# Causal attention in split precision: value products of two heads at a time, exponentials three steps ahead, and the low halves of the outputs added by VectorE

## The chip, the cores and the metric

The kernel runs on one core of a Trainium2 chip. The time is device microseconds of one execution; three executions of the kernel before were timed, and one more was recorded by the hardware profiler. The engines are TensorE (PE in the profile), its weight loads (PEld), VectorE (DVE), ScalarE (ACT), GpSimd (POOL), and SyncE (SP), which starts the DMAs.

## What is computed

A trunk of two layers over 1024 tokens of width 1024, in float32. The first layer splits its input projection between latent attention and a state-space branch; the second is gated linear attention. Only the attention of the first layer is touched:

```
q = (rms_norm(cq) @ w_uq)      -> 8 heads of 64 + 32 rotary columns
k, v from rms_norm(ckv) @ w_ukv, 8 heads of 64 each, shared rotary key of 32
s = (q_nope @ k_nope.T + q_rope @ k_rope.T) * 96**-0.5, causal
o = softmax(s) @ v             -> (1024, 8*64)
o_mla = o * silu(g_mla)
y = concat(o_mla, o_s5) @ w_out
x1 = layer_norm(alpha * x + y)
```

## The kernel before, in words

**Steps.** Attention runs over 64 steps n. A step is one tile i of 128 queries and one head h; pair p holds the tiles 2p and 2p + 1, and n = 16p + 2h + t for the tile 2p + t. The scores of a step are 128 queries by (i + 1) x 128 keys. Steps with i < 4 (n < 32, pairs 0 and 1) are SHORT: their scores fit one PSUM bank. The others take two banks.

**What happens to one step**, each item on another engine, in this order:

- "s": PE multiplies queries and keys (L2028) and adds the causal bias in the last block (L2032). VectorE takes the negated row maximum (`score_max`, L1678).
- `exponentials`: ScalarE turns the scores into probabilities in SBUF, with the row sum (L1247). This frees the score bank.
- "pt": PE transposes the probabilities block by block into bank 4 or 5 (L1950). ScalarE copies them in a rounded form, the high part (L1286); VectorE subtracts that from the same bank to get the low part (L1753). This frees the bank.
- "av": for both tiles of a head at once PE multiplies the high and the low part of the probabilities by the head's values (L2168). The stationary operand is 128 columns wide: 64 high and 64 low columns of the values, for an odd head in the opposite order. An even head writes columns 0 to 255 of bank 7, the odd head after it columns 256 to 511. So 64 of the 128 output rows are the product with the high halves of the values and the other 64 that with the low halves, and both have to be added.

**An output turn** ends each two heads, 16 times (j = 0 to 15), at the steps in `OUTPUT_TURNS` (6, 10, ..., 30, then 32, 36, ..., 60). In it VectorE scales the gate rows by the inverse sums (`gate_scaled`, L1710 and L1712); PE transposes them into bank 6 ("gT", L1950 on gate); ScalarE copies these to gateT (L1295) and bank 7 to o_parts (`output_parts`, L1268). PE multiplies o_parts by a matrix of shifted ones and adds the result to bank 7 ("ob", L2177 and L2179): this brings the low halves to the rows of the high ones. VectorE multiplies the sum in bank 7 by gateT and writes OT, which shares memory with gate (`output_gated`, L1722 and L1723). Only then is bank 7 free for the next "av".

**Other work in the loop.** "q" multiplies out the queries of later tiles (L1941) and "qT" transposes them; both use bank 6, as "gT" does. GpSimd turns the queries (L729 to L734), splits the values (L1040), and later splits the weights of the output projection (L1022, L1023). `mix_hi_tile` and `mix_lo_tile` split gated outputs for that projection.

**What sets the order.** One generator, `attention_steps`, gives the order of the items; PE, ScalarE and VectorE each run through it and issue in order what is theirs. `PsumPlan` gives each job its bank and semaphore: PE waits in `claim` until the job before on that bank is drained. The items between one "pt" and the next were placed by hand. Before, the exponentials of step n + 1 are issued around the high part of step n, and the high part of the even step that reuses one of three cells waits for the value product that read it (`values_done`).

**Behind the loop** PE runs the last "av" and "gT", the output projection of tile 0 ("z0", 36 products), and then the last "ob". SyncE waits until the last `output_gated` has drained bank 7 before it loads the weights of the layer norm into ln_gb (L907), which lies over o_parts and gateT. GpSimd applies them (L1065, L1066), and PE transposes the result.

## Time and profile before

| | us |
|---|---|
| median of three runs | 938.72 |
| lowest and highest | 937.49, 941.99 |
| the profiled execution | 938.28 |
| its span | 936.6 |
| PE busy in the span | 856.3 (91%) |
| VectorE busy | 596.9 (64%) |
| ScalarE busy | 381.6 (41%) |
| GpSimd busy | 258.1 (28%) |

The time is that of the whole execution, the span that from the first to the last instruction recorded. The mean clock that TensorE was granted is 0.966 of full speed; 1.0 stands for 2.4 GHz and 0.5 for 1.2 GHz. Attention takes the stretch from about 200 to 432 us. Busy shares over the whole span say little of one stage, so the rows below are read stage by stage. A matmul's end is modelled: where PE is full, what one instruction costs is read from one start to the next.

### The profile page before, as it was taken

The numbers are of one execution on the slowest core, as the hardware profiler recorded it, in microseconds if no ns is written. First come the engines' busy times: TensorE is split into PE (matmuls) and PEld (weight loads), VectorE is DVE, ScalarE is ACT, GpSimd is POOL, SyncE is SP. The second block draws the span as 40 slices with busy tenths as digits, with TensorE's granted clock in tenths as the row PEclk, the third lists the DMA queues.
The fourth block names the chain that finished last, engine by engine and source line by source line (L and its number), as shares of the span: only waits on it lengthen the run. The fifth ranks groups of instructions, "written<-read, shape, count | busy, mean of one in ns | idle before, by whom it ended". The sixth has DMA issues, their size and how long they took to land.

```text
span 936.6 us, 12171 instructions
## 1 busy us (share of the span) xinstructions
PE 856.3 (91%) x4136; PEld 679.3 (73%) x4136; DVE 596.9 (64%) x983; ACT 381.6 (41%) x731; POOL 258.1 (28%) x259
## 2 busy tenths in 40 slices
PE   7999999987777989998899899999899999999995
PEld 6898775755445666667787588888678888888884
DVE  6988789455444676773687154368996676654453
ACT  6253325654344555661323265325433546221120
POOL 2000002612020182000696633001955013142243
PEclk9999999996798999998999999999999999999998
DMA  9011265000000030003422311033733223012111
GB/s 330 23 28 41 70 86 119 24 3 1 1 1 1 1 113 1 1 1 116 132 90 91 112 45 46 1 112 102 213 113 123 79 68 136 23 65 71 46 45 67
DMA packets 40685, 64.19 MB, mean 69 GB/s; under 512 B 8256, under 2 KB 21824, under 8 KB 40608
## 3 DMA queue, kind: packets, MB, share of 16 engines
q1 hardware_dynamic: 40624, 63.42, 22.4%
q8 instruction: 33, 0.54, 0.2%
q14 instruction: 28, 0.23, 0.1%
HBM read 52.33 MB, written 9.44 MB: 66 GB/s over the span
## 4 chain that ended last, share of the span: by engine, by line
PE 58%; DVE 22%; ACT 7%; issue 7%; DMA 3%; POOL 1%; SPq 1%; DVEq 0%; ACTq 0%; POOLq 0%
PE psum L1941 32%; PE psum L2255 15%; PE psum L1950 4%; PE psum L2028 4%; DVE probT_lo L1753 2%; DVE negmax L1678 2%; PE psum L2168 2%; DMA ln_gb<-ln_b_dram 1%; PE psum L1976 1%; ACT probT_hi L1286 1%; ACT prob L1247 1%; DVE vg_lo L1813 1%; DMA wgs_raw<-even_w_in_dram 1%; DMA xT_raw<-x_cols_dram 1%; DVE x_lo_raw L1845 1%
## 5 line engine op out<-in xcount | busy, mean ns | idle before, releaser
L1753 DVE TENSOR_TENSOR probT_lo<-psum,probT_hi 128x512 fp32r<-128x512 f32 (+2 forms) x96 | 53.5, 558 | 63.1 <-ACT probT_hi L1286 60.8
L2255 PE MATMUL psum<-vg_hi,x1T_hi 128*128 128x512 f32 x208 | 82.1, 395 | 5.5 <-DVE vg_lo L1813 5.5
L2255 PE MATMUL psum<-vg_lo,x1T_hi 128*128 128x512 f32 x208 | 81.7, 393 | 0.0
L2255 PE MATMUL psum<-vg_hi,x1T_lo 128*128 128x512 f32 x208 | 81.6, 392 | 0.0
L2028 PE MATMUL psum<-kT,qTt 96*128 96x512 f32 (+2 forms) x192 | 79.8, 529 | 0.1
L1286 ACT ACTIVATE probT_hi<-psum 128x512 fp32r<-128x512 f32 (+2 forms) x96 | 47.1, 490 | 63.1 <-PE psum L1950 59.8
L1678 DVE TENSOR_REDUCE negmax<-psum 128x1 f32<-128x128 f32 (+3 forms) x64 | 48.5, 758 | 22.5 <-PE psum L2032 21.2
L1247 ACT ACTIVATE prob<-psum,negmax 128x128 f32<-128x128 f32 (+3 forms) x64 | 47.4, 740 | 32.5 <-issue 25.9
L2168 PE MATMUL psum<-probT_hi,V 128*128 128x256 f32 (+1 forms) x160 | 44.2, 307 | 14.2 <-DVE gate L1723 9.7
L1950 PE MATMUL psum<-ident,prob 128*128 128x128 f32 x288 | 48.5, 299 | 9.4 <-DVE probT_lo L1753 5.3
L1065 POOL TENSOR_TENSOR zn<-zn,ln_gb 128x512 f32<-128x512 f32 x16 | 23.1, 1443 | 106.9 <-DMA ln_gb<-ln_b_dram 92.6
L2168 PEld LDWEIGHTS psum<-probT_hi,V 128*128 128x128 f32 x160 | 33.5, 209 | 24.0 <-DVE gate L1723 15.7
L1941 PE MATMUL psum<-w_out_hi,Y1T_hi 128*128 128x512 f32 x128 | 50.6, 395 | 0.0
L2028 PEld LDWEIGHTS psum<-kT,qTt 96*128 96x128 f32 x192 | 35.9, 210 | 20.1 <-issue 16.4
L2255 PEld LDWEIGHTS psum<-vg_hi,x1T_hi 128*128 128x128 f32 x208 | 39.3, 189 | 15.1 <-DVE vg_lo L1813 6.8
L1941 PE MATMUL psum<-w_out_hi,Y1T_lo 128*128 128x512 f32 x128 | 49.9, 390 | 0.0
L1941 PE MATMUL psum<-x1T_hi,wqk_lo 128*128 128x512 f32 x128 | 49.9, 390 | 0.0
L1941 PE MATMUL psum<-x1T_lo,wqk_hi 128*128 128x512 f32 x128 | 49.9, 390 | 0.0
L1941 PE MATMUL psum<-w_out_lo,Y1T_hi 128*128 128x512 f32 x128 | 49.9, 389 | 0.0
L1941 PE MATMUL psum<-x1T_hi,wqk_hi 128*128 128x512 f32 x128 | 49.8, 389 | 0.0
L1950 PEld LDWEIGHTS psum<-ident,prob 128*128 128x128 f32 x288 | 33.5, 151 | 19.8 <-issue 9.8
L2255 PEld LDWEIGHTS psum<-vg_hi,x1T_lo 128*128 128x128 f32 x208 | 39.5, 190 | 8.2
(404 smaller groups left out, 2201.3 us busy)
## 6 DMA issues: line engine op xcount, KB each, us to landing
vg_piece<-odd_w_in_dram SPq DMA_DIRECT2D x60, 256.0 KB, 3.2
x_res<-x_dram SPq DMA_DIRECT2D x8, 512.0 KB, 4.2
wqk_raw<-odd_w_in_dram SPq DMA_DIRECT2D x8, 512.0 KB, 5.1
x_scratch<-zn SPq DMA_DIRECT2D x8, 512.0 KB, 2.9
w_out_raw<-odd_w_out_dram SPq DMA_DIRECT2D x4, 1024.0 KB, 5.0
V<-x_scratch SPq DMA_DIRECT2D x8, 512.0 KB, 4.6
out_dram<-SG SPq DMA_DIRECT2D x8, 512.0 KB, 2.9
xT_raw<-x_cols_dram SPq DMA_DIRECT2D x7, 512.0 KB, 8.6
```

The source lines that it names most:

```text
L1065: step(pool.tensor_tensor(zn[:, i % 2, s], zn[:, i % 2, s], ln_gb[:, 0, s], ALU.mult))
L1247: step.frees(act.activation(prob[:, place:place + (i + 1) * P], src, ACT.Exp, bias=negmax[:, n % 4:n % 4 + 1], accum_out=rsum[:, i % 2, h: ...
L1286: step(act.activation(hi, source, ACT.Copy), prob_hi_set)
L1678: step(vec.tensor_reduce(negmax[:, n % 4:n % 4 + 1], scores(n)[0], AX_X, ALU.max, negate=True), max_set)
L1753: step.frees(vec.tensor_tensor(lo, source, hi.bitcast(F32), ALU.subtract), ("pt", number))
L1813: step(vec.tensor_tensor(vg_lo[n % 3][:, :], vg_raw(n), vg_hi[n % 3][:, :].bitcast(F32), ALU.subtract), vg_split)
L1845: step(vec.tensor_tensor(lo, hi, a_lo, ALU.add), rows_summed)
L1941: mm = pe.matmul(out, lhsT, rhs, start=(k == 0), stop=(k == len(pairs) - 1))
L1950: mm = pe.transpose(bank(*job)[0:rows, k * P:k * P + cols], block_in, identity[0:cols, 0:cols])
L2028: mm = pe.matmul(psum[:, slot + part, 0:c1 - c0], qTt[:, i % 2, h, :], kT[:, h, c0:c1], start=True, stop=not diag, skip_group_check=diag)
L2168: mm = pe.matmul(bank("o", n // 2)[:, c0 + t0 * P:c0 + 2 * P], V[k][:, h // 2, 2 * (h % 2):2 * (h % 2) + 2, :].rearrange("p s d -> p (s d) ...
L2255: mm = pe.matmul(bank(*job), lhsT, rhs, start=(k == 0 and j == 0 and product not in ADDS_TO), stop=(k == 3 and j == len(pairs) - 1), skip_ ...
```

## The change

- **Low halves.** The shift matrix, o_parts and the step "ob" on PE go. `output_parts` copies only the low halves from bank 7, each to the rows of its high halves (o_low, two copies of 64x256). `output_gated` adds them to the high halves in the bank (two instructions of 64x256, into o_sum) and multiplies o_sum by gateT in one instruction of 128x256. The name "ob" stays for the job of the odd head on bank 7.
- **Value products in the short pairs.** Both heads of a turn are multiplied out in one place, ahead of "pt" at n = 5, 9, 13, ..., 29 and 32, where before each had a place of its own (n = 3, 5, 7, ...). Their places in the long pairs stay.
- **Output turns.** "gT" moves behind the scores of its step in all pairs. In the short pairs `gate_scaled` moves to the end of the step before and `output_gated` behind the low part of the step after. `output_parts` moves behind the high parts.
- **Exponentials.** In the short pairs those of step n + 3 follow the high part of step n; in the long pairs they stay as they were.
- **Queries.** The places of "q" and "qT" move by a step or so.

```diff
-        o_parts = at("o_parts", ln_at, [P, 512], F32R)
+        o_low, o_sum = at("o_low", ln_at, [P, 2 * P]), at("o_sum", ln_at + 512, [P, 2 * P])
...
         def values_turn(n):
-            return n > 2 and n % 2 == int(n in SHORT)
+            if n == len(SHORT) or n % 4 == 1 and n in SHORT:
+                return ((n - 4) // 4 * 2, (n - 4) // 4 * 2 + 1)
+            if n % 2 == 0 and n - 2 not in SHORT:
+                return (n - 2) // 2,
+            return ()
+        def queries_at(p, r):
+            places = (3, 4, 5, 7) if p else (0, 1, 3, 4)
+            if p < 3 and r in places:
+                return (2 * p + 2 + places.index(r) // 2, places.index(r) % 2),
+            return ()
...
             for n, (i, h) in enumerate(heads):
                 p, r = divmod(n, 16)
-                if values_turn(n):
-                    yield "av", (n - 2) // 2
+                for m in values_turn(n):
+                    if m >= 0:
+                        yield "av", m
                 yield "pt", n
-                if n in OUTPUT_TURNS:
-                    yield "gT", OUTPUT_TURNS.index(n)
-                    yield "ob", OUTPUT_TURNS.index(n)
-                if p and r in (1, 2):
-                    yield "qT", (2 * p + r - 1, 1)
-                if p < 3 and r in (10, 11):
-                    yield "qT", (2 * p + r - 8, 0)
-                if p < 3 and r in ((3, 5, 6, 7) if p else (0, 1, 2, 3)):
-                    nth = ((3, 5, 6, 7) if p else (0, 1, 2, 3)).index(r)
-                    yield "q", (2 * p + 2 + nth // 2, nth % 2)
+                if p and r in (0, 1):
+                    yield "qT", (2 * p + r, 1)
+                if p < 3 and r in (9, 11):
+                    yield "qT", (2 * p + 2 + (r == 11), 0)
+                for key in queries_at(p, r):
+                    yield "q", key
                 if n + 4 in SHORT:
                     yield "s", n + 4
                 if n + 2 < len(heads) and n + 2 not in SHORT:
                     yield "s", n + 2
+                if n in OUTPUT_TURNS:
+                    yield "gT", OUTPUT_TURNS.index(n)
             yield "av", STEPS - 1
             yield "gT", STEPS // 2 - 1
             yield "z0", 0
-            yield "ob", STEPS // 2 - 1
...
             def output_parts(j):
-                plan.filled(act, ("o", j))
-                step.frees(act.activation(o_parts[:, :], bank("o", j), ACT.Copy), ("o", j))
+                plan.filled(act, ("ob", j))
+                step(act.activation(o_low[0:VD, :], bank("o", j)[VD:P, 0:2 * P], ACT.Copy))
+                step.frees(act.activation(o_low[VD:P, :], bank("o", j)[0:VD, 2 * P:4 * P], ACT.Copy), ("o", j))
...
                 elif what == "pt":
-                    if n % 2 == 0 and n >= 4:
+                    if n % 2 == 0 and n + 1 not in SHORT:
                         exponentials(n + 1)
-                    if n in OUTPUT_TURNS:
-                        output_parts(OUTPUT_TURNS.index(n))
...
                         step(act.activation(hi, source, ACT.Copy), prob_hi_set)
-                    if n % 2 and 4 <= n + 1 < len(heads):
+                    if 4 <= n + 3 and n + 3 in SHORT:
+                        exponentials(n + 3)
+                    if n % 2 and n + 1 < len(heads) and n + 1 not in SHORT:
                         exponentials(n + 1)
+                    if n in OUTPUT_TURNS:
+                        output_parts(OUTPUT_TURNS.index(n))
...
-            step(vec.tensor_copy(shift[:, 0:VD], ident[:, VD:2 * VD]))
-            step(vec.tensor_copy(shift[:, 2 * VD:3 * VD], ident[:, 0:VD]))
-            step(vec.tensor_tensor(shift[:, VD:2 * VD], ident[:, 0:VD], ident[:, 0:VD], ALU.subtract))
...
             def output_gated(j):
                 p, k = divmod(j, 4)
-                plan.filled(vec, ("ob", j))
+                plan.drained(vec, ("o", j))
+                src = bank("ob", j)
+                step(vec.tensor_tensor(o_sum[0:VD, :], src[0:VD, 0:2 * P], o_low[0:VD, :], ALU.add))
+                step(vec.tensor_tensor(o_sum[VD:P, :], src[VD:P, 2 * P:4 * P], o_low[VD:P, :], ALU.add))
                 plan.drained(vec, ("gT", j))
-                cols = slice(2 * p * P, 2 * (p + 1) * P)
-                src = bank("ob", j)
-                step(vec.tensor_tensor(OT[0:VD, k, cols], src[0:VD, 0:2 * P], gateT[j % 2][0:VD, :], ALU.mult))
-                step.frees(vec.tensor_tensor(OT[VD:P, k, cols], src[VD:P, 2 * P:4 * P], gateT[j % 2][VD:P, :],
+                step.frees(vec.tensor_tensor(OT[:, k, 2 * p * P:2 * (p + 1) * P], o_sum[:, :], gateT[j % 2][:, :],
                                              ALU.mult), ("ob", j))
...
                 elif what == "pt":
-                    if n in OUTPUT_TURNS:
+                    if n in OUTPUT_TURNS and n not in SHORT:
                         gate_scaled(OUTPUT_TURNS.index(n))
-                    if n - 1 in OUTPUT_TURNS:
+                    if n - 1 in OUTPUT_TURNS and n - 1 not in SHORT:
                         output_gated(OUTPUT_TURNS.index(n - 1))
...
                         step.frees(vec.tensor_tensor(lo, source, hi.bitcast(F32), ALU.subtract), ("pt", number))
+                    if n + 1 in OUTPUT_TURNS and n + 1 in SHORT:
+                        gate_scaled(OUTPUT_TURNS.index(n + 1))
+                    if n - 1 in OUTPUT_TURNS and n - 1 in SHORT:
+                        output_gated(OUTPUT_TURNS.index(n - 1))
...
-                elif what == "ob":
-                    plan.claim(pe, ("ob", n))
-                    pe.matmul(bank("ob", n)[0:VD, 0:2 * P], shift[:, 0:VD], o_parts[:, 0:2 * P],
-                              start=False, stop=True, skip_group_check=True)
-                    pe.matmul(bank("ob", n)[:, 2 * P:4 * P], shift[:, VD:3 * VD], o_parts[:, 2 * P:4 * P],
-                              start=False, stop=True, skip_group_check=True).then_inc(plan.full(("ob", n)), 1)
```

## Rows read from the trace of the kernel before

**Rows 1.** By stretch: start:end length, busy PE, PEld, DVE, ACT, POOL, clock, DMA, GB/s.

```profile
199.90:214.71 14.81, 11.59 (x59) 7.90 (x59) 8.61 (x22) 8.90 (x28) 7.56 (x14) 0.98 0.00 1
214.71:226.29 11.58, 8.97 (x34) 6.60 (x34) 5.00 (x14) 4.34 (x14) 3.21 (x3) 0.50 0.01 1
226.29:237.47 11.18, 8.33 (x34) 5.58 (x34) 5.80 (x13) 4.35 (x14) 0.00 (x0) 0.78 0.00 0
237.47:251.18 13.71, 9.94 (x44) 5.94 (x44) 7.55 (x14) 5.84 (x14) 0.00 (x0) 0.77 0.00 0
251.18:268.07 16.89, 13.52 (x58) 9.11 (x58) 6.65 (x13) 7.52 (x17) 2.80 (x6) 0.88 0.00 1
268.07:282.33 14.26, 10.49 (x54) 6.73 (x54) 7.13 (x13) 6.54 (x15) 2.75 (x6) 0.88 0.00 1
282.33:294.95 12.62, 8.82 (x46) 6.78 (x46) 6.15 (x11) 6.05 (x14) 0.00 (x0) 0.86 0.01 1
294.95:305.94 10.99, 10.06 (x51) 7.15 (x52) 4.90 (x9) 5.48 (x12) 0.00 (x0) 0.84 0.00 0
```

**Rows 2.** Tile gate, its groups (ns min/median/max), then who waited (us, times).

```profile
L1712 DVE TENSOR_TENSOR gate<-gate,rinv x16: 424/426/2432, 212.0 to 429.6; 128x256 f32<-128x256 f32 x16
L1723 DVE TENSOR_TENSOR gate<-psum,gateT x16: 427/427/428, 214.3 to 441.8; 64x256 f32<-64x256 f32 x16
...
  PEld psum L2168: 15.7, 10
  PEld psum L1950: 12.5, 10
```

**Rows 3.** Tile o_parts: the copy's group, then who waited for it.

```profile
L1268 ACT ACTIVATE o_parts<-psum x16: 597/597/598, 211.9 to 433.3; 128x512 fp32r<-128x512 f32 x16
...
  PEld psum L2177: 6.6, 8
```

**Rows 4.** Timeline of PE in pair 1 (start, us, instruction, [idle before]).

```profile
269.56 1.46 PE L1941 MATMUL psum<-w_uq,cT 128*128 128x384 f32 x4
270.85 1.02 PE L2028 MATMUL psum<-kT,qTt 96*128 96x512 f32 x2
...
271.77 0.50 PE L1950 MATMUL psum<-ident,prob 128*128 128x128 f32 x3
272.10 0.81 PE L2028 MATMUL psum<-kT,qTt 96*128 96x384 f32 x2
...
272.78 0.36 PE L2168 MATMUL psum<-probT_hi,V 128*128 128x256 f32 x1
...
273.75 0.62 PE L1950 MATMUL psum<-ident,prob 128*128 128x128 f32 x4
274.21 1.02 PE L2028 MATMUL psum<-kT,qTt 96*128 96x512 f32 x2
```

**Rows 5.** Timeline, the turn at 381 us.

```profile
381.89 0.33 PE L2177 MATMUL psum<-o_parts,shift 128*64 128x256 f32 x1 [0.71 <-ACT o_parts L1268]
...
382.18 1.67 PE L2028 MATMUL psum<-kT,qTt 96*128 96x512 f32 x4
```

**Rows 6.** Timeline, GpSimd and VectorE at 346 us.

```profile
346.71 2.34 POOL L1023 TENSOR_TENSOR w_out_lo<-w_out_raw,w_out_hi 128x1024 fp32r<-128x1024 f32 x1
...
346.90 2.43 DVE L1712 TENSOR_TENSOR gate<-gate,rinv 128x256 f32<-128x256 f32 x1
```

**Rows 7.** Timelines of VectorE, GpSimd and PE behind attention.

```profile
441.31 0.42 DVE L1722 TENSOR_TENSOR gate<-psum,gateT 64x256 f32<-64x256 f32 x1 [11.24 <-PE psum L2179]
...
447.67 0.81 DVE L1462 TENSOR_SCALAR zn<-zn,stat 128x1024 f32<-128x1024 f32 x1
...
448.80 1.53 POOL L1065 TENSOR_TENSOR zn<-zn,ln_gb 128x512 f32<-128x512 f32 x1 [92.58 <-DMA ln_gb<-ln_b_dram]
...
451.79 0.66 PE L1950 MATMUL psum<-ident,zn 128*128 128x128 f32 x4 [2.39 <-POOL zn L1066]
...
453.75 0.63 PE L1941 MATMUL psum<-w_out_hi,OT_lo 128*128 128x512 f32 x1
```

More of the change, by code:

```diff
@@ L270, in hybrid_trunk @@
         OT_lo = at("OT_lo", RC + 4096, [P, H * VD // P, S], F32R)
-        o_parts = at("o_parts", ln_at, [P, 512], F32R)
+        o_low, o_sum = at("o_low", ln_at, [P, 2 * P]), at("o_sum", ln_at + 512, [P, 2 * P])
         gateT = [at(f"gateT{s}", ln_at + 1024 + 256 * s, [P, 2 * P]) for s in range(2)]
-        shift = at("shift", RB + 7168, [P, 3 * VD], F32R)
         gs5_lo = at("gs5_lo", D6, [P, 2, S], F32R)
@@ L489, in scores @@
             return psum[:, b0:b0 + len(score_banks(n)), :].rearrange("p a b -> p (a b)")[:, 0:w], b0 * 512
-        OUTPUT_TURNS = [4 * j + (6 if 4 * j + 5 in SHORT else 4) for j in range(STEPS // 2 - 1)]
+        OUTPUT_TURNS = [4 * j + (6 if 4 * j + 6 in SHORT else 4) for j in range(STEPS // 2 - 1)]
         def values_turn(n):
-            return n > 2 and n % 2 == int(n in SHORT)
+            if n == len(SHORT) or n % 4 == 1 and n in SHORT:
[8 more added lines that the diff above has]
+            return ()
         def attention_steps():
@@ L530, in hybrid_trunk @@
                     plan.give(("pt", number), 4 + number % 2)
-            elif what == "av" and n % 2 == 0:
-                plan.give(("o", n // 2), 7)
-            elif what == "ob":
-                plan.give(("ob", n), 7)
+            elif what == "av":
+                plan.give(("ob" if n % 2 else "o", n // 2), 7)
             elif what == "z0":
@@ L710, in hybrid_trunk @@
         for m, g in cell_users:
-            if m % 2 == 0 or (m, g + 1) in cell_of:
+            if (m, g + 1) in cell_of:
                 value_turns[m, g] = len(value_turns) + 1
@@ L718, in values_done @@
             else:
-                plan.filled(engine, ("o", m // 2))
+                plan.filled(engine, ("ob" if m % 2 else "o", m // 2))
         def prob_blocks(n, number, first, blocks):
@@ L902, in _ @@
                 if i == 1:
-                    plan.filled(sp, ("o", STEPS // 2 - 1))
+                    plan.filled(sp, ("ob", STEPS // 2 - 1))
                     wqk_load(0)
@@ L2173, in _ @@
                         if k == 2 * p + 1 or k % 4 == 3:
-                            mm.then_inc(pv_done if (n, k // 4) in value_turns else plan.full(("o", n // 2)), 1)
-                elif what == "ob":
-                    plan.claim(pe, ("ob", n))
-                    pe.matmul(bank("ob", n)[0:VD, 0:2 * P], shift[:, 0:VD], o_parts[:, 0:2 * P],
-                              start=False, stop=True, skip_group_check=True)
-                    pe.matmul(bank("ob", n)[:, 2 * P:4 * P], shift[:, VD:3 * VD], o_parts[:, 2 * P:4 * P],
-                              start=False, stop=True, skip_group_check=True).then_inc(plan.full(("ob", n)), 1)
+                            mm.then_inc(pv_done if (n, k // 4) in value_turns
+                                        else plan.full(("ob" if h % 2 else "o", n // 2)), 1)
                 elif what == "gT":
```

## The prediction

> **What bounds the kernel now.** I went from the page's 40 slices (the granted clock leaves full speed in the slices that belong to attention's first half) to the view by stretches, cut at each end of L1723, the last instruction of an output turn [rows 1]. A step is one query tile of one head; each row but the first and the last is four steps, the first seven, the last two. Steps 0 to 15 are pair 0 (128 and 256 keys), steps 16 to 31 pair 1 (384 and 512). The reader should see that no other engine is full in these eight rows, and that behind the first the clock is granted at 0.50 to 0.88: VectorE (DVE) is busy 5.00 of 11.58 us, 5.80 of 11.18, 7.55 of 13.71, 6.65 of 16.89, ScalarE (ACT) no more. TensorE (PE) looks busy because at half clock its instructions last longer. So the stretch from 200 to 306 us is a chain of waits. Who waits for whom is in the view of the tile gate [rows 2]: the weight loads of the value products wait 15.7 us in ten places for L1723, those of the gate transposes 12.5 us in ten for L1712; and the shift products 6.6 us in eight for ACT's copy [rows 3]. The order of the work makes it: gate scaling, transpose, copy, shift product and gating stand within one step, each on another engine, and the next value product is queued right behind on PE.
>
> **The sum is against the profiled execution,** 938.28 us (span 936.6), which is 0.44 below the median of 938.72.
>
> **Removed: the shift product and its copy.** Sixteen pairs of products go. A pair costs PE 0.29 us of queue (381.89 to the next score product at 382.18) and before it the wait, 0.71 there [rows 3, 5]. ACT's copy of 128x512, 0.597, becomes two of 64x256; the nearest row is the 128x256 copy of gateT, 0.38, so ACT pays 0.8 for 0.6: +0.2 per turn. The three constants for the shift at 170 us go too; nothing waits for them, and I count nothing.
>
> **Added on DVE.** Before: two products of 64x256, 0.43 each (L1723; L1722 is like it) [rows 2]. After: two adds of the same shape and sources, and a product of 128x256 from two SBUF tiles, like L1712, 0.43. So +0.45 per turn, 7 us in 16 turns; it costs nothing where DVE has idle time, which it has in all short rows, and its full size where DVE is the late one.
>
> L1712 took 2.43 us once, at 346.90, with GpSimd's split running from 346.71 to 349.05 [rows 6]: the new product can be held up as L1712 was. Two turns (L1722 at 336 and 352 us now) lie beside those splits: at worst 2 us each, at best nothing; I take 1.5 us together. The Trainium skill (SBUF — State Buffer, "SBUF: two separate sides") says that a VectorE instruction with two SBUF inputs and a GpSimd instruction exclude each other for a whole instruction. By it the two adds, which read PSUM, are safe and the product is not; the old gating, PSUM times SBUF, was never exposed. The L1712 row agrees for its kind; the sum above stands on the row alone.
>
> **Moved, in the short pairs.** Gate scaling goes a step earlier (after the low part of step 5, 9, ...), the transpose behind the score of step 6, 10, ..., the gating behind the low part of step 7, 11, ..., and the value products of both heads to step 9, 13, .... The wait for L1712 should vanish: half a step or more now lies between. The wait for the gating shrinks, since a transpose and a score product stand before the value product, but does not vanish. Exponentials run three steps ahead instead of one, so that transposes no longer wait for ACT. What is late next: DVE's run of low part, three gating instructions, maximum; then ACT, where the exponential of n+3 sits between the high parts of n and n+1 and waits for a maximum queued behind the gating.
>
> Full-clock cost on PE, start to start [rows 4]: query product 1.29, score of 512 keys 0.92, of 384 keys 0.68, transposes of three blocks 0.33 and of four 0.46, value product 0.97. Four steps of pair 1: 2 x (0.92 + 0.68 + 0.33 + 0.46 + 0.97) + 0.25 for the gate = 7.0 us. With the queries in between (some 0.5 per turned half, an estimate from 0.11 a block): 237.47 to 251.18: 8; to 268.07: 7.0 + 4 x 1.3 = 12.2; to 282.33: 9; to 294.95, where two steps have no score: 6; the two steps to 305.94, with five and six blocks: 6. Sum 41 us against 68.5 on the clock. The best of these rows now runs at 16.89/12.2 = 1.38 times its need, with its stalls. I take 1.35 for all: 55.5 us, **gain 13**. Bounds: 1.2 (gain 19) and 1.55 (gain 5). DVE's busy time, 32.4 us plus 5 x 0.45, stays below in each case.
>
> Pair 0: the two four-step rows take 22.8 us. If only DVE counted they would be 5.0 + 0.45 and 5.8 + 0.45, some 6 us each; if PE stayed at half clock, its busy time there, 9.0 [rows 1], is nearly full. I take 8.5 each, since an engine that has to stop for latencies will see the lower clock again: gain 5.8 (between 4 and 10). The first seven steps lose one wait of L1723 and one of L1712 and keep four query products: 1.2. **Gain 7.**
>
> **Long pairs (306 to 432 us).** The turn at 381 us [rows 5]: the score product comes 1.0 us sooner (0.71 + 0.29), so the maximum that waits for it can start some 0.8 sooner. Behind it on DVE stand gating and the low part of the next step, and for these the value product waits. Gating is 0.45 longer: 0.4 remains. Seven turns: 2.8. If DVE has no slack beside it: minus 0; if PE is the late one: up to 7. Less the 1.5 above: **gain 1.3.**
>
> **Behind attention.** The last shift product stands behind 36 products of the output projection; DVE sits idle 11.24 us for it until 441.31, and only then are the layer norm's weights asked for; GpSimd waits for them until 448.80, PE for GpSimd 2.39 us until 451.79, and PE then runs eight products at 1.2 GHz (0.63 us each, starts some 0.4 apart) [rows 7]. After: the gating ends near 435.5 (copy 433.3 to 434.1, then 1.3), the weights come 6.7 us sooner, and the layer norm of tile 0 is late next: now it takes 6.3 us for two halves (from 442.2, behind the gating, to 448.5, the end of L1462 [rows 7]); its first half can run early then, and behind the second, which comes at 441, I estimate 4.7 us. With GpSimd's 2.9 (two instructions like the 1.53) this gives 448.6, against PE arriving at 449.1. So 0.3 + 2.4 + 1.4 (seven starts, 0.2 each) = **gain 4** (between 1, if the clock falls anyway and the norm is late, and 5). Later DVE is the late engine, but it has idle time for PE between, which absorbs this.
>
> **Sum:** 13 + 7 + 1.3 + 4 = 25.3: 913.0 us, 2.7% less.
>
> **Rivals.** *The next wait takes over half.* In the short pairs the gating, now three instructions, and the value products of two heads in one piece starve ACT: a maximum behind the gating delays the exponential, this the high part. For it: the two queues are in order and latencies are as long as before. Against: each has over 4 us idle per turn. Short gain 10 instead of 20: 923. *The clock comes back.* If PE stays busy enough for full clock in both pairs: factor 1.2 and 7 us a turn: 19 + 10 + 2 + 4 = 35: 903. *No change:* only the tail and the shift products count, and the pairs regain nothing: 4 short of the half-percent bound, 934 or more. *Slower.* VectorE is the late engine in all turns. It gets 16 x 0.45 = 7.2 us more; two held products add 3; ACT's 16 x 0.2 adds 3 if its copies stand ahead of the high part's release; less the tail's 4: 947. It decides from the point where the gating ends later than PE's transposes and score of step 8, 12, ... by more than today's 1.6 (15.7 over ten); DVE's idle time in [rows 1] speaks against it.
>
> **How the numbers follow.** Forecast 0.46, half gain 0.26, clock 0.17, no change 0.05, slower 0.06. Half a percent, 4.7 us, is about what can be told from no change. The range 898 to 930 leaves out part of the best case, the last two and the worst part of the half gain. Faster 0.89, same 0.05, slower 0.06.
>
> **What would show it.** In the changed trace: no products with shift; no idle time before gate transposes; waits of value products for the gating under 8 us in total; the stretch from the first exponentials to the last turn of pair 1 near 86 us for 106; DVE's product of two SBUF tiles at 0.43; the layer norm's weights asked for within 4 us of the last gate transpose and PE without a gap over 1 us before the first turned norm tile; the granted clock in the short pairs above 0.8. The prediction is wrong if ACT or DVE shows over 90% busy in pair 1, or if PE waits for probabilities where it waited for the gate.

## The result, and the profile after

The changed kernel takes 917.64 us in the median of four runs (915.56 to 918.06), the kernel before 938.42 beside it (four runs, 937.49 to 941.99). The ratio is 0.9767, with a 95% interval of 0.9738 to 0.9797: 2.3% faster, some 21 us where 25 were forecast. The profiled execution is 918.06, its span 916.3, to 938.28 and 936.6 before.

The head of the page of the kernel after: engines with their busy time, then the granted clock in 40 slices.

```profile
span 916.3 us, 12152 instructions
...
PE 844.2 (92%) x4104; PEld 672.6 (73%) x4104; DVE 602.0 (66%) x996; ACT 384.3 (42%) x747; POOL 257.4 (28%) x259
...
PEclk9999999998989999989999799999999999999998
```

VectorE has 5 us more work and TensorE shows 12 us less, which is clock as well as removed products. The totals don't say where the time went; the stretches do. The view by stretches of the kernel after, cut at the end of each gating as in [rows 1], same columns:

```profile
199.90:216.33 16.43, 11.52 (x65) 8.02 (x63) 9.22 (x23) 10.52 (x34) 9.55 (x16) 0.98 0.00 1
216.33:225.86 9.53, 7.99 (x36) 6.15 (x36) 5.42 (x15) 4.51 (x15) 1.14 (x1) 0.67 0.01 2
225.86:234.45 8.59, 6.35 (x34) 3.84 (x34) 6.23 (x15) 5.37 (x15) 0.00 (x0) 1.00 0.00 0
234.45:244.82 10.37, 7.75 (x37) 4.93 (x38) 8.24 (x16) 6.22 (x15) 0.00 (x0) 0.92 0.00 0
244.82:259.19 14.37, 13.06 (x64) 8.53 (x63) 7.18 (x14) 7.84 (x19) 3.40 (x8) 0.94 0.01 2
259.19:270.50 11.31, 8.70 (x49) 5.90 (x48) 7.56 (x15) 6.07 (x15) 2.16 (x5) 0.85 0.00 1
270.50:280.77 10.27, 8.01 (x44) 6.45 (x42) 6.58 (x13) 4.98 (x11) 0.00 (x0) 0.84 0.01 2
280.77:288.11 7.34, 6.30 (x44) 5.21 (x45) 5.32 (x10) 4.08 (x10) 0.00 (x0) 1.00 0.00 0
```

The last gating of pair 1 ends at 288.11 where it ended at 305.94: 17.8 us. Every row but the first is shorter; the first is 1.6 longer, since the gating that closes it now stands behind the low part of the next step. The clock is 0.67 to 1.00 behind the first row, where it was 0.50 to 0.88. Time spent at half clock, worked out as twice (1 - clock) times the length and summed over these seven rows, falls from 37.3 us to 16.4.

Tile gate of the kernel after, groups and waiters as in [rows 2]:

```profile
L1718 DVE TENSOR_TENSOR gate<-gate,rinv x16: 424/425/1269, 210.8 to 410.5; 128x256 f32<-128x256 f32 x16
L1729 DVE TENSOR_TENSOR gate<-o_sum,gateT x16: 424/426/2120, 215.4 to 415.9; 128x256 f32<-128x256 f32 x16
...
  PEld psum L2178: 16.3, 10
...
  PEld psum L1960: 4.2, 5
```

The wait of the gate transposes (L1960; L1950 before) fell from 12.5 us to 4.2. That of the value products (L2178; L2168 before) for the gating did not fall at all over the whole of attention: 15.7 to 16.3. It fell in the short pairs, from 12.2 to 8.0, and grew behind them from 3.5 to 8.2 (the tile's view from 306 us on before, from 288 us on after). The view of waits, from 216 to 288 us, of the kernel after (who, for whom, us in total, times, longest):

```profile
DVE probT_lo L1759 <- ACT probT_hi L1291: 20.4, 14, 3.0
...
ACT probT_hi L1291 <- PE psum L1960: 11.0, 8, 2.6
ACT prob L1253 <- DVE negmax L1687: 10.2, 9, 2.1
PEld psum L2178 <- DVE gate L1729: 8.0, 5, 3.8
...
PE psum L1960 <- ACT gateT L1304: 4.2, 3, 2.0
```

The third line is new: in the same view of the kernel before, from 215 to 306 us, ScalarE's exponential waits for no maximum. One turn shows how it comes about. The chain of waits of the kernel after, from 258 us (start, us, what), in order of time:

```profile
259.66 1.88 PE psum L2178 x16
261.54 0.47 PE psum L1960 x4
...
262.10 0.61 ACT probT_hi L1291
...
262.80 0.70 DVE probT_lo L1759
263.52 0.19 DVE rinv L1716
263.74 0.43 DVE gate L1718
264.19 0.70 DVE qTt L1681
264.92 0.70 DVE negmax L1687
...
265.69 0.07 ACT prob L1253
...
266.50 0.39 ACT o_low L1274
266.92 0.38 ACT o_low L1275
267.32 0.39 ACT gateT L1304
...
267.85 1.06 PE psum L1960 x4
```

The maximum (L1687) stands on VectorE behind the low part, the gate scaling and a query copy. ScalarE waits for it, and behind that exponential, of a step that is needed three steps later, stand the copies of the outputs and of the gate, and PE's transposes of the queries, which share bank 6 with the gate, wait for the last of them. No engine is full here; four engines hand one piece of work round.

Behind attention, timeline of the kernel after (start, us, engine, instruction, idle before), to be read beside [rows 7]:

```profile
415.03 0.42 DVE L1726 TENSOR_TENSOR o_sum<-psum,o_low 64x256 f32<-64x256 f32 x1 [4.11 <-ACT o_low L1275]
...
416.40 0.34 SPq L913 DMA_DIRECT2D ln_gb<-ln_g_dram  x1
...
425.95 0.81 DVE L1471 TENSOR_SCALAR zn<-zn,stat 128x1024 f32<-128x1024 f32 x1
...
426.93 1.71 POOL L1071 TENSOR_TENSOR zn<-zn,ln_gb 128x512 f32<-128x512 f32 x1 [88.71 <-DVE zn L1471]
...
430.13 0.66 PE L1960 MATMUL psum<-ident,zn 128*128 128x128 f32 x4
```

The weights of the layer norm are asked for at 416.40, 3.4 us behind the last gate transpose (412.99), and GpSimd now waits for the norm (L1471) instead of for them. PE shows no idle time before the first turned norm tile.

### The profile page after: what moved, and what is told of

Read it like the earlier page. It is cut to its first block, busy times and chain, and to the rows that moved or that the text cites. A ratio compares the mean times of both kernels' runs of the same rounds, so it can differ in the third digit from the quotient of the medians.

```text
span 916.3 us, 12152 instructions
## 1 busy us (share of the span) xinstructions
PE 844.2 (92%) x4104; PEld 672.6 (73%) x4104; DVE 602.0 (66%) x996; ACT 384.3 (42%) x747; POOL 257.4 (28%) x259
## 4 chain that ended last, share of the span: by engine, by line
PE 56%; DVE 23%; ACT 9%; issue 6%; DMA 3%; SPq 1%; POOL 1%; DVEq 0%; ACTq 0%; POOLq 0%
PE psum L1951 32%; PE psum L2260 14%; DVE probT_lo L1759 3%; PE psum L1960 3%; PE psum L1986 3%; DVE negmax L1687 2%; PE psum L2178 2%; ACT probT_hi L1291 2%; ACT prob L1253 2%; PE psum L2038 1%; DVE vg_lo L1823 1%; DMA wgs_raw<-even_w_in_dram 1%; DVE stat L1467 1%; DVE gate L1729 1%; DVE x1T_lo L1782 1%
## 5 line engine op out<-in xcount | busy, mean ns | idle before, releaser
L2038 PE MATMUL psum<-kT,qTt 96*128 96x512 f32 (+2 forms) x192 | 75.1, 501 | 0.1
L2178 PE MATMUL psum<-probT_hi,V 128*128 128x256 f32 (+1 forms) x160 | 43.9, 306 | 13.2 <-DVE probT_lo L1759 6.8
L1687 DVE TENSOR_REDUCE negmax<-psum 128x1 f32<-128x128 f32 (+3 forms) x64 | 48.5, 758 | 10.4 <-PE psum L2042 8.4
L1960 PE MATMUL psum<-ident,prob 128*128 128x128 f32 x288 | 45.9, 289 | 10.0 <-DVE probT_lo L1759 8.7
L2178 PEld LDWEIGHTS psum<-probT_hi,V 128*128 128x128 f32 x160 | 33.7, 211 | 20.0 <-DVE gate L1729 16.3
L2038 PEld LDWEIGHTS psum<-kT,qTt 96*128 96x128 f32 x192 | 33.6, 197 | 19.3 <-issue 15.9
L1960 PEld LDWEIGHTS psum<-ident,prob 128*128 128x128 f32 x288 | 33.2, 147 | 18.2 <-issue 15.5
```

What stands on the lines that cost most here:

```text
L1687: step(vec.tensor_reduce(negmax[:, n % 4:n % 4 + 1], scores(n)[0], AX_X, ALU.max, negate=True), max_set)
L1960: mm = pe.transpose(bank(*job)[0:rows, k * P:k * P + cols], block_in, identity[0:cols, 0:cols])
L2038: mm = pe.matmul(psum[:, slot + part, 0:c1 - c0], qTt[:, i % 2, h, :], kT[:, h, c0:c1], start=True, stop=not diag, skip_group_check=diag)
L2178: mm = pe.matmul(bank("o", n // 2)[:, c0 + t0 * P:c0 + 2 * P], V[k][:, h // 2, 2 * (h % 2):2 * (h % 2) + 2, :].rearrange("p s d -> p (s d) ...
```

## The experiments

Three lengths from each trace carry the argument: **short**, from the end of the gating of turn 0 to that of turn 7; **long**, from there to turn 14; **tail**, from the last gate transpose to the end of the last instruction. "Half clock" is worked out as above, summed over the seven turns of the short stretch. These lengths come from one profiled execution of each kernel, which can lie up to 2.2 us from the median. How much they say can be read from two pairs that run the same code up to the last gate transpose: before and e6_tail are 1.5 us apart in the short stretch and 0.6 in the long one, e10_order_only and e11_order_tail less than 0.1 in both.

| kernel | median | ratio to before, 95% | short | long | last gate transpose | tail | half clock |
|---|---|---|---|---|---|---|---|
| before | 938.42 | 1 | 91.2 | 113.3 | 432.1 | 504.4 | 37.3 |
| after | 917.64 | 0.9767 (0.9738-0.9797) | 71.8 | 112.0 | 413.0 | 503.4 | 16.4 |
| e1_near | 907.91 | 0.9679 (0.9656-0.9703) | 63.1 | 112.0 | 404.1 | 503.4 | 6.9 |
| e8_shift_kept | 913.67 | 0.9738 (0.9714-0.9763) | 68.4 | 108.5 | 406.3 | 504.6 | 6.8 |
| e2_low_only | 946.03 | 1.0069 (1.0045-1.0093) | 97.4 | 115.8 | 442.8 | 502.7 | 48.3 |
| e6_tail | 936.54 | 0.9982 (0.9962-1.0001) | 92.7 | 113.9 | 434.5 | 500.2 | 41.0 |
| e9_two_ahead | 908.53 | 0.9657 (0.9641-0.9672) | 63.3 | 113.2 | 405.4 | 499.2 | 3.4 |
| e10_order_only | 905.43 | 0.9625 (0.9610-0.9641) | 61.4 | 108.6 | 398.1 | 504.1 | 0 |
| e11_order_tail | 902.86 | 0.9610 (0.9584-0.9637) | 61.4 | 108.6 | 397.8 | 503.8 | 0 |
| e12_dve_plus | 907.57 | 0.9649 (0.9632-0.9666) | 63.9 | 110.7 | 402.6 | 505.1 | 3.4 |
| e13_gate_places | 927.08 | 0.9862 (0.9836-0.9887) | 81.4 | 111.1 | 419.7 | 504.1 | 20.5 |
| e14_av_apart | 908.80 | 0.9671 (0.9647-0.9694) | 66.2 | 108.5 | 402.0 | 504.5 | 3.4 |
| e16_order_tail_two | 903.51 | 0.9629 (0.9598-0.9659) | 62.6 | 108.5 | 397.9 | 503.9 | 3.4 |
| e17_old_queries | 905.38 | 0.9636 (0.9611-0.9661) | 66.3 | 107.1 | 400.7 | 504.2 | 6.8 |

The experiments ran on three chips: the kernel before took 939.5 in the median beside e1, e2, e6 and e8, 940.93 beside e9 to e12, 940.77 beside the rest, and 938.42 beside the change. So medians are subtracted only within such a group, and across groups the ratios or the lengths are compared.

### e1_near: the change, with the exponentials one step ahead as before

```diff
-                    if 4 <= n + 3 and n + 3 in SHORT:
-                        exponentials(n + 3)
-                    if n % 2 and n + 1 < len(heads) and n + 1 not in SHORT:
+                    if n % 2 and 4 <= n + 1 < len(heads):
                         exponentials(n + 1)
```

> The changed kernel, but in the short pairs the exponentials stand where they stood before: those of step n + 1 ahead of the high part of an even step n and behind that of an odd one. Theory A (order and exponentials share the gain of the short pairs): the transposes of probabilities wait for ScalarE again, 8.8 us in ten places there in the kernel before, and the high part queues behind an exponential; some 7 us of the 18 that the turns up to 306 us gained are lost, 925 us. Theory B (the order of turns and value products did all of it): 918, no more than 1.5 off. Theory C (only the exponentials count): 932 or more.

Measured: 907.91, ratio 0.9679 to the change's 0.9767. The short stretch is 8.7 us shorter (63.1 for 71.8), the long one the same to 0.01 us. None of the three theories has this: all took the exponentials further ahead for a help or for nothing, and they are a loss.

### e8_shift_kept: the change, with the shift product and o_parts as before

```diff
-                step(act.activation(o_low[0:VD, :], bank("o", j)[VD:P, 0:2 * P], ACT.Copy))
-                step.frees(act.activation(o_low[VD:P, :], bank("o", j)[0:VD, 2 * P:4 * P], ACT.Copy), ("o", j))
+                step.frees(act.activation(o_parts[:, :], bank("o", j), ACT.Copy), ("o", j))
...
+                for at_ in OUTPUT_TURNS:
+                    if n == at_ + int(at_ in SHORT):
+                        yield "ob", OUTPUT_TURNS.index(at_)
```

VectorE's adds go with it.

> The new order and the far exponentials, with the low halves still brought over by TensorE's shift products (in short pairs one step behind the transposed gate, in long pairs right behind it, the last one behind the 36 output products). Theory A: the tail's 4.2 us and some 3 us in the long pairs (0.7 of wait and 0.3 of products a turn, less VectorE's 0.45) are lost, the short pairs keep nearly all: 926 us; first wait in the tail is VectorE for the last shift product again, 10 us or more. Theory B (VectorE's adds cost in the short pairs what they save): 922. Theory C (the adds are the main gain): 932 or more.

Measured: 913.67, ratio 0.9738. Against the change the lengths shrink by 3.4 and 3.5 us (68.4 for 71.8, 108.5 for 112.0), and all three theories asked for more than 920. Beside far exponentials the adds that take the shift product's place cost 0.5 us in each turn, in long pairs as in short ones; with near ones (e1_near against e10_order_only) the short stretch loses 1.6. What they bring back lies in the tail only.

### e2_low_only: the kernel before, with VectorE's adds for the shift products and nothing else

```diff
+                step(vec.tensor_tensor(o_sum[0:VD, :], src[0:VD, 0:2 * P], o_low[0:VD, :], ALU.add))
+                step(vec.tensor_tensor(o_sum[VD:P, :], src[VD:P, 2 * P:4 * P], o_low[VD:P, :], ALU.add))
...
-                elif what == "ob":
```

> The kernel before, with the low halves added by VectorE and no shift products, all places in the order as before. Theory A: tail 4.2 and long pairs 1.3 as in the changed kernel, and in the short pairs the wait for the copy goes (0.4 to 0.7 a turn) while the gating gets 0.45 longer right ahead of the value product that waits for it, so about nothing there: 933 us. Theory C (adds are the main gain): 925 or less. If the longer gating costs more than the copy's wait did: 936 or more.

Measured: 946.03, 0.69% slower than before (0.45 to 0.93), as in the last of the three cases expected. The short stretch is 6.2 us longer, where seven turns times 0.45 us of added VectorE work make 3.2, and the long one 2.5. On the old order, where PE already waits for the gating, the short turns pay for the added work about twice; the time at half clock grows with it, from 37.3 to 48.3 us.

### e6_tail: the kernel before, with the last shift product ahead of the 36

```diff
-            yield "z0", 0
             yield "ob", STEPS // 2 - 1
+            yield "z0", 0
```

> The kernel before, with the last shift product ahead of the output projection of tile 0. Theory A: TensorE waits about 1.1 us more for ScalarE's copy there, VectorE is free some 7 us sooner, the weights of the norm come sooner, and no gap of 2.4 us nor the half clock behind it: 935.5 us, 3 less than before. Rival (the norm of tile 0 is as late for another reason): 938 to 940, with the gap in TensorE still there.

Measured: 936.54, ratio 0.9982 (0.9962 to 1.0001); 3.0 less by the medians, 4.2 by the tails of the traces (500.2 for 504.4). The same edit on e10_order_only is e11_order_tail, 2.6 less by the medians, though only 0.3 by the two traces. One line gets most of what the new gating gets behind attention.

### e9_two_ahead: the change, with the exponentials two steps ahead

```diff
-                    if 4 <= n + 3 and n + 3 in SHORT:
-                        exponentials(n + 3)
+                    if 4 <= n + 2 and n + 2 in SHORT:
+                        exponentials(n + 2)
```

> The changed kernel with exponentials two steps ahead in the short pairs (n + 2 behind the high part of n) instead of three. Theory D: three ahead costs 10 us because the exponential of n + 3 needs a maximum that VectorE takes only behind the gating, and ScalarE's next high part stands behind that exponential (10.2 us of such waits in nine places in the changed kernel, none with the near ones). Two ahead, the maximum is a step older: those waits are under 2 us and the time is 908 to 910. Rival E: what helps is that near exponentials come in pairs, then two high parts; two ahead, one by one, stays at 915 to 918.

Measured: 908.53, short 63.3, as good as one step ahead and as theory D has it. Waits of e9_two_ahead from 216 to 280 us, same columns as above:

```profile
ACT probT_hi L1291 <- PE psum L1960: 15.0, 9, 3.1
DVE probT_lo L1759 <- ACT probT_hi L1291: 13.0, 11, 2.5
PEld psum L2178 <- DVE gate L1729: 7.8, 6, 2.5
```

No wait of an exponential for a maximum is left in that view, and VectorE waits 13.0 us for the high part instead of 20.4; the wait for the gating stays (7.8 to 8.0). So what costs is not that exponentials run ahead but that the third step's maximum is not there when ScalarE comes to it. e8_shift_kept, three ahead without the adds, has the line too:

```profile
ACT prob L1260 <- DVE negmax L1693: 12.2, 11, 1.7
```

### e10_order_only and e11_order_tail: the new order alone

The first is e8_shift_kept with the exponentials of e1_near; the second adds the edit of e6_tail.

> The new order of turns, value products and queries alone: shift products kept, exponentials as before. If the three parts add up (907.9 for near exponentials, 3.9 less for the shift kept): 904 us. If far exponentials hurt only together with the longer gating: 908 to 914.

> The same, with the last shift product ahead of the 36 output products. The traces of the kernel before and of the one with only this edit give 4.2 us from the last transposed gate to the end: 900 us. If the norm of tile 0 is late for another reason: 904.

Measured: 905.43 and 902.86; the first is near the sum of the parts (904), the second lies between its two cases. The order alone takes 29.8 us from the short stretch and 4.7 from the long one, and no half clock is left in the short stretch. A part of the long gain shows in the timeline of e10_order_only, a turn of pair 2, for [rows 5]:

```profile
349.72 1.67 PE L2045 MATMUL psum<-kT,qTt 96*128 96x512 f32 x4
...
351.02 0.60 ACT L1281 ACTIVATE o_parts<-psum 128x512 fp32r<-128x512 f32 x1
...
351.29 0.39 PE L1967 MATMUL psum<-ident,gate 128*128 128x128 f32 x2
...
351.67 0.33 PE L2194 MATMUL psum<-o_parts,shift 128*64 128x256 f32 x1
```

The four score products now stand ahead of the gate transposes and the shift product, and the copy is done while they run: the shift product follows the transposes without an idle time of PE. The 0.71 us wait of [rows 5] is gone from this turn although the shift product is still there; over the long stretch PE's waits for that copy fall from 3.9 us in six places to 1.6 in two.

### e12_dve_plus: e10_order_only with one more VectorE instruction in each gating, its result unused

```diff
+                step(vec.tensor_tensor(unused[0:VD, :], src[0:VD, 0:2 * P], gateT[j % 2][0:VD, :], ALU.mult))
```

> Order only, with one more VectorE instruction of 64x256 (0.42 us, result unused) at the head of every gating: VectorE's extra time of the adds, without the adds. Theory F: the adds cost time because VectorE's gating is on the path in all turns: 16 x 0.45 = 7 less what idle time hides, 909 to 911, and long pairs 0.5 us a turn longer. Rival G: the cost is in ScalarE's two copies or in bank 7 coming free later through them: 904 to 906 here.

Measured: 907.57, 2.1 more than e10_order_only by the medians. An instruction of 0.42 us costs 2.4 us in the seven short turns and 2.1 in the seven long ones, 0.3 us a turn; the last gate transpose comes 4.5 us later. The change with near exponentials (e1_near) is 6.0 us later there. By the ratios the shares are less clear, 0.0024 of 0.0054: the profiled execution of e12_dve_plus is the slowest of its four, that of e10_order_only the fastest, and up to 1.7 of the 2.4 us may be the clock (3.4 us at half clock for none). The time, 907.57, lies between theory F (909 to 911) and rival G (904 to 906).

The long stretch is the place to tell the two apart, since it repeats to 0.1 us over e8, e10, e11, e14 and e16 (108.5 to 108.6). There the extra instruction costs 2.1, the adds 3.5, and VectorE instructions held up beside GpSimd's splits (last section) last 2.7 us longer than usual in e1_near, 1.7 in e10_order_only and 1.5 in e12_dve_plus. Counted one for one, that takes 1.0 us off the adds' price, and 2.4 are left against 2.2 for the instruction: here it is VectorE's longer gating, and little is left for ScalarE's 0.16 us more per turn. For the short stretch this was not taken apart.

### e13_gate_places, e14_av_apart, e17_old_queries: which part of the order

e13_gate_places is the kernel before with the gate scaled a step earlier in the short pairs, and gate transpose and shift product behind the score products everywhere:

```diff
-                if n in OUTPUT_TURNS:
-                    yield "gT", OUTPUT_TURNS.index(n)
-                    yield "ob", OUTPUT_TURNS.index(n)
                 if p and r in (1, 2):
...
                     yield "s", n + 2
+                if n in OUTPUT_TURNS:
+                    yield "gT", OUTPUT_TURNS.index(n)
+                    yield "ob", OUTPUT_TURNS.index(n)
```

> The kernel before with one part of the new order: the gate is scaled a step earlier in the short pairs, and its transpose and the shift product stand behind the scores of their step in all pairs. Value products, gating, exponentials and queries stay. Theory H (the long pairs' gain is this alone): turns 7 to 14 take 108.5 us as in the order-only kernel, for 113.3, and the short ones gain only the waits for L1712, some 6 us: 929. Rival (the short pairs' gain is mostly here, through the clock): 915 or less.

e14_av_apart is e10_order_only with the value products of the two heads at steps 8 and 9, 12 and 13, ... instead of together at 9, 13, ...:

```diff
-            if n == len(SHORT) or n % 4 == 1 and n in SHORT:
+            if n == len(SHORT):
                 return ((n - 4) // 4 * 2, (n - 4) // 4 * 2 + 1)
+            if n % 4 < 2 and n in SHORT:
+                return (n // 4 * 2 - 2 + n % 4,)
```

> Order only, but with the value products of the two heads a step apart in the short pairs (ahead of the transposes of steps 8 and 9, and so on, where both stood ahead of 9). The gating they wait for ends behind the low part of step 7, so the first of them stands a transpose and a score product closer to it and holds both up. Theory: 0.5 to 1.5 us per turn more, 909 to 914. If two value products in one piece starve ScalarE more than that: 905 or less.

e17_old_queries is e10_order_only with the query products and transposes where they stood before:

```diff
-            places = (3, 4, 5, 7) if p else (0, 1, 3, 4)
+            places = (3, 5, 6, 7) if p else (0, 1, 2, 3)
```

> Order only, with query products and their transposes at the places of the kernel before. They share bank 6 with the transposed gate, and a transpose of queries right behind it waits for ScalarE's copy of the gate. Theory: the places matter little, 905 to 907, up to 1 us in each of two or three turns. If they make the gain of the short pairs: 912 or more.

Measured: the places of the gate alone give 9.9 us of the short stretch and 2.2 of the long one (927.08). Theory H is wrong for the long pairs (111.1 for the 108.5 it asked for) and low for the short ones. From there to e14_av_apart, with the gating and the value products a step or two later, ScalarE's copy of the outputs behind the high parts and the queries' new places, it is 15.2 more in the short stretch, and joining the two heads another 4.8 (some 4 by the ratios). The queries' new places shorten the short stretch by 4.9 in these two traces, where e17_old_queries has 6.8 us at half clock and e10_order_only none; they cost 1.5 in the long one, and the ratios, 0.9636 and 0.9625, don't tell the two kernels apart. Both times came out about as expected, 908.80 for 909 to 914 and 905.38 for 905 to 907.

The 1.5 us is one gate scaling in another place beside GpSimd's split; e10_order_only, then e17_old_queries:

```profile
318.24 2.08 DVE L1725 TENSOR_TENSOR gate<-gate,rinv 128x256 f32<-128x256 f32 x1
...
321.29 0.67 DVE L1725 TENSOR_TENSOR gate<-gate,rinv 128x256 f32<-128x256 f32 x1
```

In e13_gate_places it takes 2.42 us. So of the 4.1 us between e13_gate_places and e17_old_queries in the long stretch 1.8 is that wait. Their orders differ there in one thing only, the copy of the outputs, which e17_old_queries has behind the high parts; some 2.3 us stand against it, by elimination, since no run moved the copy alone.

### e16_order_tail_two: e11_order_tail with the exponentials two ahead

The edit is that of e9_two_ahead.

> The order with the last shift product ahead of the output products, and exponentials two ahead in the short pairs. With longer gating two ahead was as fast as near ones (63.3 us for seven turns against 63.1), so 902 to 904; if the pairing of near exponentials costs once the gating is short: 899 or less.

Measured: 903.51, ratio 0.9629 (0.9598 to 0.9659), the last gate transpose at 397.88 for 397.84. Two steps ahead gain nothing over one, as expected. **The best version is e11_order_tail,** 902.86: 3.9% under the kernel before (3.6 to 4.2), and by the ratios 1.6% under the change.

## Why the prediction was right in sum and wrong in its parts

**The sum.** From the traces: short pairs 17.8 (20 forecast), long pairs 1.3 (1.3), then behind the last gate transpose 4.2 up to the fourth norm tile (4). That is 23.4 to the forecast's 25.3. In the profiled executions 3.2 us of it are given back later, in the second layer; the last section says how. In the short pairs the split is near too: first seven steps -1.6 for +1.2 (the gating moved out behind them), pair 0 4.6 for 5.8, pair 1 14.8 for 13, that is a factor of 53.7/41 = 1.31 for the 1.35 taken. A reader who stopped here would call every step right. That the sum came out is luck in good part: the order gave more than was forecast (29.8 us in seven turns), and the two other parts, taken for a help and for nearly free, took 10.3 of it back in the short pairs.

**Far exponentials: the sign was wrong.** The step "Exponentials run three steps ahead instead of one, so that transposes no longer wait for ACT" took them for a help. They cost 8.7 us. What they remove is small: in e1_near, with them near, transposes wait 2.3 us (PE) and 5.1 (PEld) for an exponential. What they bring was named in the same paragraph, an exponential that "waits for a maximum queued behind the gating", and then given no price of its own: it is 10.2 us of waits in nine places. Without the adds the same step costs 7.0 (e8_shift_kept against e10_order_only).

**The order was undersized.** With those 8.7 us and the adds taken away, the order gives 29.8 us in the short stretch. That is the rival in which the clock comes back, whose short gain I put at 19 + 10: pair 1 takes 47.5 us in e10_order_only, 1.16 times its need, below the 1.2 that I took as the best bound. The factor was read from a row of the old order, which still had waits in it; it was no limit.

**Long pairs: a right number from two wrong ones.** The step has +0.4 a turn from the shift product less 1.5. The runs show +4.7 from the new order, which I counted as nothing (2.2 of it from the gate transpose and shift product behind the scores, e13_gate_places, and most of the rest, by elimination, from the copy of the outputs behind the high parts), and -3.5 from VectorE's adds (e8_shift_kept against the change, the same again e10_order_only against e1_near). The failed step is "the maximum that waits for it can start some 0.8 sooner": most of the 0.71 us of [rows 5] went with the order, so little more than the 0.29 in PE's queue was left for the removed product to save, against a gating 0.45 us longer. What grew instead is the value products' wait for that gating, from 3.5 to 8.2 us behind the short pairs, where it is 1.7 in e8_shift_kept and in e10_order_only.

**The adds as a whole are a loss.** They were put at 0.45 a turn that "costs nothing where DVE has idle time". VectorE was idle for over 5 us in each short row behind the first of [rows 1], and in the rows after it is for 2.0 to 7.2; yet in e12_dve_plus one more instruction of 0.42 us costs 0.3 a turn. That idle time is the wait for the others in the ring, not slack: PE's next value products wait for the gating, VectorE's next low part for ScalarE, ScalarE for PE. The tail's 4 us is the whole return, and e6_tail gets about 3 of it by moving one item. That the adds lose is clear of noise with near exponentials (0.9679 for 0.9625); with far ones the intervals of the two ratios overlap.

**The held-up product** was right in kind, 1.7 us in one place for the 1.5 taken; four more instructions, one of them a gate scaling, last 0.2 to 0.8 us longer than usual. But the kernel before had lost 2.0 us to the same thing at 346.90 [rows 6], so over the long stretch the net loss is 0.8. The rows of the first stand in the last section.

**The marks.** Shown as forecast: the product of two SBUF tiles at 0.426, the norm's weights asked for within 4 us, no gap of PE before the first norm tile, the stretch to the last turn of pair 1 at 88.2 us (86 forecast). Missed: gate transposes still wait 4.2 us in five places, value products 16.3 (under 8 forecast; 8.0 in the short pairs), and the clock is under 0.8 in one row. And the sentence on what would make the prediction wrong asked for an engine over 90% busy or PE waiting for probabilities. Neither came, and parts of it were wrong all the same: the new wait sat on ScalarE, which is busy 48 to 60% of each row of pair 1. One reading of [rows 1] was off too, without changing the sum: in the row of 16.89 us ScalarE is busier than VectorE, 7.52 us for 6.65.

**The slower rival** (947) is what e2_low_only does: 946.03 without the order, with VectorE's adds paid for in short and long pairs. It was not the changed kernel's way, because the order brings the last gate transpose 34.0 us forward, where e2_low_only puts it 10.6 back.

## What to carry to other kernels

Engines that issue in order pay for the place of an item, not only for its length: put what waits for another engine (a gate transpose, a shift product) behind work that is ready, and look ahead only as far as the input is there. Three steps ahead put a late maximum in front of three ready copies, two did not. Idle time in a ring of engines is not slack; before work is moved to the "idle" engine, ask whether the instruction stands between two releases. And when a forecast of a bundle comes out right, run the parts: here one part gave 34 us of the way to the last gate transpose and the two others took 15 back.

## What the hardware showed

**The clock takes its share of gains and losses.** In the short stretch the time at half clock goes, roughly, with the length: 48.3 us for a length of 97.4, 37.3 for 91.2, 16.4 for 71.8, 6.9 for 63.1 (e1_near), 0 for 61.4. PE starts 302 to 321 matmuls in it each time, so what differs is waits and clock, and a wait can cost more than its own length.

**The clock gave back 3.2 us far from the change.** Windows of five us in the second layer, kernel after, then the same work in the kernel before (columns as in [rows 1]):

```profile
511.60:516.60 5.00, 3.75 (x9) 2.76 (x10) 1.05 (x3) 4.84 (x7) 4.54 (x5) 0.62 0.00 0
516.60:521.60 5.00, 5.00 (x17) 3.90 (x17) 2.50 (x3) 2.72 (x3) 0.00 (x0) 0.70 0.01 2
```

```profile
535.00:540.00 5.00, 4.01 (x17) 3.07 (x18) 0.79 (x3) 4.84 (x7) 4.62 (x5) 1.00 0.01 2
540.00:545.00 5.00, 5.00 (x24) 4.14 (x23) 2.65 (x4) 2.69 (x4) 0.00 (x0) 1.00 0.00 0
```

PE starts 26 matmuls there at clock 0.62 and 0.70, before 41 at full clock, and nothing of the change touches this place. From 90 to 108 us behind the last gate transpose the time at half clock, worked out as above, is 10.2 us in the kernel after, in e1_near and in e2_low_only, 3.4 in the one before, and none in e6_tail and e9_two_ahead, whose tails are the shortest (500.2 and 499.2 us). The 6.8 us more at half clock that the kernel after has there can cost it up to 3.4 us; 3.2 were lost. The same holds for e6_tail: of its 4.2 us up to 1.7 may be the clock, and the medians say 3. Why it falls so in one kernel and not in another was not tested.

**GpSimd holds up VectorE where both sources are SBUF.** Timeline of the kernel after at 318 us, beside [rows 6]:

```profile
317.94 2.35 POOL L1029 TENSOR_TENSOR w_out_lo<-w_out_raw,w_out_hi 128x1024 fp32r<-128x1024 f32 x1
317.99 0.43 DVE L1727 TENSOR_TENSOR o_sum<-psum,o_low 64x256 f32<-64x256 f32 x1
318.45 2.12 DVE L1729 TENSOR_TENSOR gate<-o_sum,gateT 128x256 f32<-128x256 f32 x1
```

The add, which reads PSUM, ends on time beside GpSimd's split; the product, which reads SBUF twice, ends at 320.57, 0.28 us behind the end of the split, and takes 2.12 us for 0.43. The Trainium skill (SBUF — State Buffer, "SBUF: two separate sides") tells of such an exclusion between the two engines for a VectorE instruction with two SBUF inputs; the trace agrees, both in the product (2.12 us) and in the add, which has one (0.43 us). How much a kernel loses to this hangs on which instructions happen to lie beside a split, and a change elsewhere in the order can move it by 1.4 us, as e17_old_queries shows.
